# A conformer/short-conv block on eight cores: twenty token tiles transposed by DMA instead of TensorE, a gate computed one stage later, bias adds split in two

## What is computed

```
shift1, scale1, gate1, shift2, scale2, gate2 = split(silu(c) @ w_ada + b_ada)
h  = LN(x) * (1 + scale1) + shift1
a_val, a_gate, b_gb, b_gc, b_x, g_a, g_b = split(h @ w_in + b_in)        # 7 x 1024 columns
u  = silu(LN(conv31(a_val * sigmoid(a_gate))));   y_a = u @ w_a_out + b_a_out
v  = b_gb * conv3(b_gc * b_x);                    y_b = v @ w_b_out
x1 = LN(alpha * x + (1 + gate1) * ((sigmoid(g_a) * y_a + sigmoid(g_b) * y_b) @ w_o + b_o))
h2 = LN(x1) * (1 + scale2) + shift2
y  = LN(alpha * x1 + (1 + gate2) * (relu(h2 @ w_up + b_up)^2 @ w_down + b_down))
```

## Time and profile before

| | |
|---|---|
| median of 3 runs | 1168.89 us (1168.38 to 1169.64) |
| the profiled execution's own time | 1170.01 us |
| its span (core 4, the slowest) | 1169.0 us |
| spans of the eight cores | 1155.9 to 1169.0 us |
| PE, DVE, ACT, POOL busy | 94%, 58%, 37%, 15% of the span |

### The profile page before, as it was taken

The page is one execution under the profiler, slowest core; times in us unless marked ns, Lnnn a source line. Parts: engine busy times, 40 slices in busy tenths (PEclk is TensorE's granted clock), DMA queues, the critical chain, the costliest instruction groups (busy, mean ns, idle before and its releaser), DMA issues.

```text
span 1169.0 us, 19292 instructions; the slowest of 8 cores (1155.9 to 1169.0 us)
## 1 busy us (share of the span) xinstructions
PE 1102.7 (94%) x6607; PEld 577.5 (49%) x6676; DVE 677.8 (58%) x1159; ACT 437.2 (37%) x773; POOL 175.1 (15%) x159
## 2 busy tenths in 40 slices
PE   1699999979999999999999999999999999999896
PEld 1366776434445677644444444444444444444343
DVE  4548766827653267588877767877032782210566
ACT  2344436824442234584466644456000043320000
POOL 4004011002100000111321021210060000003300
PEclk9999999989999999999999999999999999999898
DMA  9999998998555652498763685636944399654412
GB/s 189 179 138 127 136 158 116 207 188 162 74 73 93 110 90 34 60 182 160 127 127 85 132 148 117 130 75 139 223 72 72 72 187 239 106 81 74 73 56 89
DMA packets 150335, 143.14 MB, mean 122 GB/s; under 512 B 33840, under 2 KB 138688, under 8 KB 149984
## 3 DMA queue, kind: packets, MB, share of 16 engines
q0 software_dynamic: 106736, 87.73, 53.9%
q1 hardware_dynamic: 43504, 54.18, 16.7%
HBM read 203.22 MB, written 16.79 MB: 188 GB/s over the span
## 4 chain that ended last, share of the span: by engine, by line
PE 80%; DMA 6%; DVE 5%; issue 3%; ACT 3%; SPq 2%; POOL 2%; DVEq 0%; ACTq 0%; POOLq 0%
PE bank L161 79%; DMA wb<-w_in 4%; SPq L138 2%; ACT nb L1063 2%; DMA wb<-w_down 1%; POOL x1r L1286 1%; PE bank L531 1%; DVE cbuf L1055 1%; DMA u<-nb 1%; DVE slot L500 1%; DVE fT L1236 0%; ACT sg L1135 0%; DVE x L664 0%; DVE sg L1138 0%; POOL wb L138 0%
## 5 line engine op out<-in xcount | busy, mean ns | idle before, releaser
L161 PE MATMUL bank<-hT,wb 128*128 128x512 bf16 (+4 forms) x2112 | 387.9, 337 | 1.9 <-ACT sg L1135 1.3
L161 PEld LDWEIGHTS bank<-hT,wb 128*128 128x128 bf16 x2112 | 202.2, 98 | 156.8 <-issue 13.9
L161 PE MATMUL bank<-h2T,wb 128*128 128x512 bf16 x1002 | 222.8, 379 | 3.1 <-DVE x L664 1.9
L161 PE MATMUL bank<-wb,fT 128*128 128x512 bf16 x941 | 209.2, 381 | 5.4 <-DMA wb<-w_down 4.4
L161 PEld LDWEIGHTS bank<-h2T,wb 128*128 128x128 bf16 x1024 | 99.5, 98 | 121.5 <-issue 2.9
L161 PEld LDWEIGHTS bank<-wb,fT 128*128 128x128 bf16 x960 | 94.0, 98 | 118.7 <-issue 6.2
L1234 ACT ACTIVATE rr<-bank,pvec 128x512 bf16<-128x512 f32 x128 | 85.1, 683 | 111.1 <-PE bank L161 108.9
L1236 DVE TENSOR_TENSOR fT<-rr 128x512 bf16<-128x512 bf16 x128 | 63.4, 513 | 91.0 <-ACT rr L1234 91.0
L505 ACT ACTIVATE slot<-slot,eps 128x1 f32<-128x1 f32 (+1 forms) x65 | 17.6, 290 | 253.9 <-DVE slot L502 240.2
L1254 DVE TENSOR_TENSOR gt<-bank,g2b 128x512 f32<-128x512 f32 x32 | 21.9, 683 | 123.1 <-PE bank L161 123.1
L138 POOL DMA_DIRECT2D wb<-w_in x40 | 36.0, 925 | 326.3 <-PE bank L161 305.5
(11 more groups left out here) (116 smaller groups left out, 1180.8 us busy)
## 6 DMA issues: line engine op xcount, KB each, us to landing
wb<-w_in POOLq DMA_DIRECT2D x16, 1024.0 KB, 13.3
wb<-w_up POOLq DMA_DIRECT2D x16, 1024.0 KB, 13.2
wb<-w_down POOLq DMA_DIRECT2D x15, 1024.0 KB, 9.9
wada<-w_ada POOLq DMA_DIRECT2D x12, 1024.0 KB, 18.8
wb<-w_in POOLq DMA_DIRECT2D x24, 512.0 KB, 19.6
xt<-xs SPq DMA_DIRECT2D x16, 512.0 KB, 9.7
x<-xs SPq DMA_DIRECT2D x16, 512.0 KB, 5.0
x1d<-x SPq DMA_DIRECT2D x16, 512.0 KB, 3.2
```

The costliest lines, as they stand in the source:

```text
L161: inst = pe.h.matmul(out, lhsT, rhs, start=self.first, stop=last)
```

## The change

1. The 8 tiles of block 1's `hT` and tiles 0 to 5 of each block's `h2T` (20 of the 24) are transposed by one DMA each, issued on SP with `transpose=True`, from the normalised tile in SBUF straight to its place. Scale and shift are applied later, in place, by `modulate_tiles`: 5 DVE and 3 ACT instructions over a group of 3 tiles (`hT`) or 2 tiles (`h2T`). Tiles 6 and 7 of each `h2T` stay as they were. Block 1's `hT` loses its gaps, so its columns are read as one run.
2. The first weight tile of each `up` runs over tokens 0 to 511 for its four column groups and then over tokens 512 to 1023.
3. Gate 2 moves: its two `w_ada` loads to step 0 of block 1's GLU, `ada_gate` to step 14, `ada_rows` to step 16, `ada_spread` and the scaling of `b_down` to step 20.
4. In both `down`, tiles 4 to 7 get their bias at `gq == 1` and tiles 0 to 3 at `gq == 2`.

```diff
     def ada_rows(i_):
+        off = (OFF_BC, OFF_TMP + 15872)[i_]
+        grow, r_grow = sb(off, [8, 128], F32, "grow"), newres("grow%d" % i_, off, 512)
...
+    def modulate_tiles(hT, r_hT, t0, t1, sc, sh, rm):
+        for kc in range(KC):
+            view = hT[:, kc, t0 * 128:t1 * 128]
+            x_ = 0 if kc < 5 else 1
+            rw = [r_hT[t][x_] for t in range(t0, t1)]
+            if kc < 5:
+                dve.op(lambda e: e.tensor_scalar(view, view, modT[:, sc + kc:sc + kc + 1], modT[:, sh + kc:sh + kc + 1], ALU.mult, ALU.add),
+                       reads=rw + [rm], writes=rw)
+            else:
+                act.op(lambda e: e.activation(view, view, AF.Identity, bias=modT[:, sh + kc:sh + kc + 1], scale=modT[:, sc + kc:sc + kc + 1]),
+                       reads=rw + [rm], writes=rw)
...
+    def dma_transpose(dst, src, owner, reads, writes):
+        sp.deps(reads, writes)
+        if owner.dsem is None:
+            fw.nsem += 1
+            owner.dsem = nc.alloc_semaphore("d%d_%s" % (fw.nsem, owner.name))
+        owner.dcnt += 16
+        sp.h.dma_start(out=dst, in_=src, transpose=True).then_inc(owner.dsem, 16)
...
         def trans(i):
             npart, ri, dv = tiles[i]
+            if not raw:
+                dma_transpose(hT[:, :, i * 128:(i + 1) * 128], xn[i % nxn], own("tr%d" % (i % nxn)), [r_xn[i % nxn]], r_hT[ri])
+                return
...
+        def mod(g):
+            modulate_tiles(hT, r_hT[1:], 3 * g, min(3 * g + 3, NT), SC1, SH1, r_mod1)
...
         def trans(t):
-            transpose_evac(h2n[t % 2], 128, r_h2n[t % 2], h2T, r_h2T[t], lambda dst, kc: dst[:, kc, t * 128:(t + 1) * 128],
-                           (SC2, SH2, r_mod2), n_dve)
...
+            if t >= 6:
+                transpose_evac(h2n[t % 2], 128, r_h2n[t % 2], h2T, r_h2T[t], lambda dst, kc: dst[:, kc, t * 128:(t + 1) * 128],
+                               (SC2, SH2, r_mod2), n_dve)
+                return
+            dma_transpose(h2T[:, :, t * 128:(t + 1) * 128], h2n[t % 2], own("tr2_%d" % (t % 2)), [r_h2n[t % 2]], r_h2T[t])
+
+        def mod(i):
+            modulate_tiles(h2T, r_h2T, 2 * i, 2 * i + 2, SC2, SH2, r_mod2)
...
         def hcols(kc, s):
+            if b > 0:
+                return hT[:, kc, s * 512:(s + 1) * 512]
             return hT[:, kc, :].rearrange("p (r n) -> p r n", n=PW)[:, 4 * s:4 * s + 4, PW - NPH:PW]
+
+        def hbank(ap):
+            return ap if b > 0 else grp4(ap)
...
+            def hin(kc):
+                return cols(hT, kc) if b == 0 else hT[:, kc, r0_ * 128:r1_ * 128]
...
-                grp.mm(view(bank_ap[bi]), wa[:, kc, jj * 128:(jj + 1) * 128], cols(hT, kc), [ra[jj // 2]] + rd, last=(kc == KC - 1))
+                grp.mm(bank_ap[bi][:, 0:n], wa[:, kc, jj * 128:(jj + 1) * 128], hin(kc), [ra[jj // 2]] + rd, last=(kc == KC - 1))
...
         n_ = 0
         for g in range(8):
             wu, ru, iu = ws_get()
-            for jj in range(4):
+            for jj, s in ([(jj, s) for s in range(NS) for jj in range(4)] if g == 0 else [(jj, s) for jj in range(4) for s in range(NS)]):
                 fc = 4 * g + jj
-                for s in range(NS):
+                if True:
...
         for gq in range(4):
             wd, rd, idn = ws_get()
-            if gq == 2:
-                for t in range(NT):
-                    x1_bias(t)
-                if last:
+            if gq in (1, 2):
+                for t in range(4):
+                    x1_bias(t if gq == 2 else t + 4)
+                if last and gq == 2:
                     wl, rl = sb(OFF_H[1], [128, 8, 512], BF16, "wl"), newres("wl", OFF_H[1], 8192)
                     dma_group(pool, [(wl, wsrc(w_down, 3 * 1024, 512))], own("wl"), writes=[rl])
...
+        if n in (7, 14):
+            n0 = {7: 6, 14: 8}[n]
             for nt in (n0, n0 + 1):
                 ada_load(nt, OFF_H[1] + (nt % 2) * 8192, "h%d" % (nt % 2))
...
-        if n == 11:
+    plan = Plan()
+
+    def scaled_bias(c_, dst, gb_, rg_, off):
+        bst, r_bst = sb(off, [128, D], F32, "bstage"), newres("bst", off, 4096)
+        sp.dma(bst, bc_d[:, c_:c_ + 1024], own("bst"), writes=[r_bst])
+        pool.op(lambda e: e.tensor_tensor(dst, bst, gb_, ALU.mult), reads=[r_bst, rg_], writes=[r_bias])
+
+    def glu1_side(n):
+        if n == 0:
+            for nt in (10, 11):
+                ada_load(nt, OFF_CB + (nt % 2) * 8192, "h%d" % (nt % 2))
+        elif n == 14:
             ada_gate(1)
-        if n == 12:
+        elif n == 16:
             ada_rows(1)
-        if n == 15:
+        elif n == 20:
             ada_spread(1)
-
-    plan = Plan()
+            scaled_bias(5120, bdb, g2b, r_g2, OFF_TMP + 6144)
...
         r_bc2 = newres("bc", OFF_BC, 8192)
         sp.dma(bc, bc_d[:, 0:2048], own("bc"), writes=[r_bc2, r_bc])
-        bst = sb(OFF_TMP + 12288, [128, D], F32, "bstage")
-        r_bst = newres("bst", OFF_TMP + 12288, 4096)
-        for c_, dst, gb_, rg_ in ((4096, bob, g1b, r_g1), (5120, bdb, g2b, r_g2)):
-            sp.dma(bst, bc_d[:, c_:c_ + 1024], own("bst"), writes=[r_bst])
-            pool.op(lambda e: e.tensor_tensor(dst, bst, gb_, ALU.mult), reads=[r_bst, rg_], writes=[r_bias])
+        scaled_bias(4096, bob, g1b, r_g1, OFF_TMP + 12288)
...
@@ -1397,9 +1449,10 @@
                     plan.add(9 * g + 2 * i, pp["stats"], t)
                     plan.add(9 * g + 5, pp["root"], t)
                     plan.add(9 * g + 6 + 2 * i, pp["norm"], t)
-                    plan.add(9 * g + 8 + 2 * i, pp["trans"], t)
+                    plan.add(9 * g + 7 + 2 * i, pp["trans"], t)
                 if t + 6 < NT:
                     plan.add(9 * g + 7 + 2 * i, pp["load"], t + 6)
+            plan.add(min(9 * g + 14, 30), pp["mod"], g)
...
         plan.add(0, scale_wo, 15)
-        p3_plan(pp, 2, 3, (1, 2, 4, 5, 7))
-
-    def p3_plan(pp, first, step, lags):
+        p3_plan(pp, 2, 3, (1, 2, 4, 5, 7), 4)
...
             for lag, key in zip(lags, ("root1", "ln1", "root2", "ln0", "trans")):
                 plan.add(n + lag, pp[key], t)
+            if t % 2 == 1 and t < 6:
+                plan.add(n + lags[4] + mlag, pp["mod"], t // 2)
             if t + nx < NT:
                 plan.add(n + lags[3], pp["load"], t + nx)
...
-    mg1, r_mg1 = token_mix(1, side["P1"], OFF_H[0], OFF_CB + 16384, no_side, no_side, gb1_side, plan.run, after_gb1)
+    mg1, r_mg1 = token_mix(1, side["P1"], OFF_H[0], OFF_CB + 16384, glu1_side, no_side, gb1_side, plan.run, after_gb1)
     plan.done()
...
-    p3_plan(H2[1], 4, 6, (2, 4, 7, 9, 13))
+    p3_plan(H2[1], 4, 6, (2, 4, 7, 9, 13), 9)
     fT, r_fT = up(0, H2[0]["h2T"], H2[0]["r_h2T"], plan.run)
...
```

More of the change, by code:

```diff
@@ L595, in x_ring @@
         return slot, load
+    def modulate_tiles(hT, r_hT, t0, t1, sc, sh, rm):
[16 more added lines that the diff above has]
+        sp.h.dma_start(out=dst, in_=src, transpose=True).then_inc(owner.dsem, 16)
+        ev = (owner.dsem, owner.dcnt, "dma_" + owner.name)
+        for r in reads:
+            r.r["dma_%s_%d" % (owner.name, owner.dcnt)] = ev
+        for w in writes:
+            w.w = ev
+            w.r = {}
     def p1_setup(b, ring, xn_offs, raw, n_dve):
-        hT = sb(OFF_H[b], [128, KC, TW], BF16, "hT")
+        hT = sb(OFF_H[b], [128, KC, TW if raw else TB], BF16, "hT")
         _g = new_group(fw, ["hT%d_%d%s" % (b, t, ab) for t in range(NT + 1) for ab in "ab"], OFF_H[b], OFF_H[b] + HSZ)
@@ L631, in trans @@
             npart, ri, dv = tiles[i]
+            if not raw:
+                dma_transpose(hT[:, :, i * 128:(i + 1) * 128], xn[i % nxn], own("tr%d" % (i % nxn)), [r_xn[i % nxn]], r_hT[ri])
+                return
             transpose_evac(xn[i % nxn], npart, r_xn[i % nxn], hT, r_hT[ri], dv, None if raw else (SC1, SH1, r_mod1), n_dve)
-        return dict(hT=hT, r_hT=r_hT, load=load, stats=stats, root=root, norm=norm, trans=trans, n=len(tiles))
+        def mod(g):
+            modulate_tiles(hT, r_hT[1:], 3 * g, min(3 * g + 3, NT), SC1, SH1, r_mod1)
+        return dict(hT=hT, r_hT=r_hT, load=load, stats=stats, root=root, norm=norm, trans=trans, mod=mod, n=len(tiles))
     def p3_setup(b, mg, r_mg, wo, x1_offs, h2n_offs, n_dve):
@@ L688, in trans @@
         def trans(t):
-            transpose_evac(h2n[t % 2], 128, r_h2n[t % 2], h2T, r_h2T[t], lambda dst, kc: dst[:, kc, t * 128:(t + 1) * 128],
-                           (SC2, SH2, r_mod2), n_dve)
-        return dict(h2T=h2T, r_h2T=r_h2T, load=load, bias=bias, proj=proj, root1=root1, ln1=ln1, root2=root2, ln0=ln0, trans=trans, nx1=nx1)
+            if t >= 6:
[5 more added lines that the diff above has]
+            modulate_tiles(h2T, r_h2T, 2 * i, 2 * i + 2, SC2, SH2, r_mod2)
+        return dict(h2T=h2T, r_h2T=r_h2T, load=load, bias=bias, proj=proj, root1=root1, ln1=ln1, root2=root2, ln0=ln0, trans=trans, mod=mod, nx1=nx1)
     class Plan:
@@ L908, in pair @@
             for kc in range(KC):
```

(7 more changed lines are left out.)

11 lines of the change are left out of this document (3 added, 8 removed).

## The result

The changed kernel takes **1153.01 us** (median of 4 runs, 1152.17 to 1153.36) against 1169.27 of the kernel before (4 runs, 1168.38 to 1170.01). The ratio is 0.986, with a 95% interval of 0.9843 to 0.9877: faster, by 16.3 us. The forecast was 1145 and a gain of 23.6. The time lies inside the range of 1139 to 1163, but 2 us above the likeliest case (1139 to 1151), in the band that the prediction gave to rival (a), that the holes close only in part. Only fast runs are compared, those in which neither die fell to a lower clock than the other; one run of the kernel before at 1189.37 us still counts as fast and lowers the ratios of one chip, that of the repeat and the three kernels after it, by some 0.2%.

A forecast was written before the change was run, and what follows sets the result against it. TensorE, busy 94% of the span, was taken as the bound. Transposes 9.0, gate 7.7, bias adds 6.9, `up` 1.0, less 1.0 for XC, gave 23.6: 1170.0 to 1146.4, median 1145 us; range 1139 to 1163.

The forecast's parts named there:

- rival (a): The holes at the first `u` group and last `down` close only in part: about 15 us gained, 1154; chance 0.2.
- the stall for `u` and what follows: Block 0's first `u` group: 6.0 us hole plus 1.9 of slow clock go, less 1.5 for late pieces.
- row matmuls and gate: TensorE's wait ahead of the row matmuls before block 0's merge goes with gate 2's move: 1.3 us.
- wait in XC: Start of block 1's XC: ACT may wait for staging bytes shared with `cbf`; cost 1.0 us, bounds 0 and 4.
- bias adds: Last `down`: last weights load 4.6 us sooner, closing a 4.44 us hole and its 2.5 us after-effect; 6.9 us.
- The gate's step: Taking gate 2's 2.1 MB from ahead of the `u<-nb` pieces shortens the queue by 12 us, against a 6.04 us hole.
- Rival (b): Slow DMA transposes stall TensorE, from 10.4 us a tile in block 0's merge, 13.8 beside `w_o`; 1216 at 16; chance 0.12.
- 20 tiles x 0.45 = 9.0 us: Both merges and `up(0)`: each tile not transposed on TensorE saves 0.45 us of path, 9.0 us in all.
- The first goes with DVE's evictions: `up(0)`: TensorE's 1.9 us wait for `x` goes, its 0.8 us wait for `h2n` stays; 1.0 us booked.
- The check on core 5: Core 5's 1160.6 us less 9.0, 1.3 and some 5 for its smaller holes gives 1145, agreeing with the forecast.
- rival (c): New waits of many kinds eat the gains up to nothing, within 0.2%; chance 0.03.

The follow-up runs named there:

- the repeat: The changed kernel run again, unaltered, on the chip of the next three kernels: ratio 0.9838, median 1156.81 us.
- the three kernels after it: The changed kernel with gate 2's staging load, row and multiplication earlier (1155.67 us), with `h2T` scaling later (1152.83), and with the two together (1151.39).
- the doubled run: The changed kernel with every transposing DMA issued twice, SP waiting for the first: 1168.99 us, ratio 0.9957.
- both edits: The changed kernel with gate 2's staging load, row and multiplication earlier and `h2T` scaling later in merge 1 and `up(0)`: 1151.39 us, ratio 0.9791.
- The last run: Against the kernel with both edits, seven instead of three of a tile pair's eight scale-and-shift instructions on ScalarE in `up(0)`: 1148.54 us, ratio 0.979.

## Why the prediction was nearly right, and where it failed

The table sets the terms against core 4, the core for which they were worked out.

| term | booked | measured on core 4 |
|---|---|---|
| transposes, 8 tiles in block 0's merge | 3.6 | 3.6 |
| transposes, 6 tiles in merge 1 | 2.7 | 0.5 |
| transposes and `x` waits, `up(0)` | 3.7 | 1.5 |
| the stall for `u` and what follows | 6.4 | 8.1 |
| row matmuls and gate (GB of block 0, GLU of block 1) | 1.3 | 0.6 |
| wait in XC | -1.0 | -0.4 |
| bias adds | 6.9 | 7.1 |
| sum | 23.6 | 21.0 |

- **The gate's step was right.** The stall is gone on every core of the changed kernel, and the groups behind it keep 1.73 us. The two terms of block 0's merge add to the 11.7 us of the stage table and are split by the run with the gate alone (8.1) and the two runs with and without `hT` (3.6). The 1.5 us kept back for late pieces weren't needed.
- **The bias adds were right**: 60.43 us up to `wl` is 280 matmuls at 0.216, without a hole. The margin of the last load was booked as 0.65 us, with 16 us to land; it landed in 12.8 on core 7, 3.9 us ahead of its use.
- **A DMA transpose** takes 5.0 to 5.1 us by the medians of core 7 (3.8 to 5.6 over the cores), against 6 taken from the pace of the `u<-nb` pieces; the ends of 1.6 and 39 us were far off. No engine waits for one. By the 1309 ns for one 128x128 block of the Trainium skill, "VectorE: DVE Perf Modes", section "The three transpose paths", a tile of eight would take 10.5 us, an estimate. By the 261 GB/s of the Trainium skill, "DMA: Bandwidth & Descriptors", section "Latency and other measured facts", it would take about 1 us, also an estimate. Both miss the median; 10.6 and 11.2 us were seen in the crowd, 3.0 at the least.
- **Rival (b)'s threshold** left something out. Behind the place of the scaling it gave TensorE three steps of free banks, 10.4 us. Measured are 4.9: the 28.3 us that TensorE bears less the 23.4 at which the scaling stands. The rows of the doubled run fit with that: when the scaling is late, ScalarE has 2.30 us of it, two table loads and the square roots to do, 5.6 us from 306.10 to 311.67, before it reads the next bank, and three steps of 3.45 us less 5.6 leave 4.8. The 10.4 us a tile "without end" was a pace over many groups; no run measured that.
- **The step that failed:** "20 tiles x 0.45 = 9.0 us, and this is path, since TensorE has no slack there". The price of 0.45 is exact, and eight tiles gave it in full. For twelve it went again into new holes, because the scaling that comes back in was costed at nothing ("covered by those engines' spare time"). On core 4, merge 1 won 2.7 us and lost 2.1 to a hole that it did not have; `up(0)` won 2.7, but where three holes of 2.7 us in all had been, one of 2.3 us now stands, and the clock of 0.72 behind it costs some 1.7 more (16 matmuls from 754.74 to 759.88 us take 5.1 instead of 3.45). The spare time is an average over stages. In merge 1 the cover was there but the place wrong: 2.3 us of VectorE ahead of the chain that tile 7 needs; moved two steps, the whole 2.7 us came (130.39). In `up(0)` the cover isn't there. VectorE is busy 103.1 of 142 us there even with both edits, in one chain with ScalarE and the banks, and the DMA took only 0.9 us of work from it (24 evictions, 8.2 us before; 5.2 us of scaling and 2.1 of evictions after). It is GpSimd's additions that make VectorE the bound, as the run without them shows: 139.03 us and no hole. The last run agrees: 12 scalings less on VectorE shorten the stage by 3.35 us.
- **"The first goes with DVE's evictions"** failed with it: the waits on `x` grew from 1.9 to 5.1 us.
- **The check on core 5** (1160.6 less 15.3) failed for the same reason. Core 5 got 8.6 us in block 0's merge in all, 2.1 in the last `down` and 0.5 in merge 1, and lost 1.0 in `up(0)`, 0.7 in XC and 0.5 at the start: 9.0, so that it ended at 1151.6.
- **Not booked at all:** a stage that was equal on all cores and becomes uneven costs the slowest core more than the mean. XC (up to +2.3), `up(0)` (2.5 between cores) and the start (2.8 us later on core 7 than in the execution before, by nothing that the change touched) came together on core 7. The clock behind the new holes belongs here too: it fell on some cores, for 1.7 us each time. Between the 1146.4 forecast for the profiled execution and its own time of 1153.36 lie 7.0 us: 2.6 are core 4's missing terms, 4.3 its distance to core 7 (1152.3 - 1148.0).
- **Luck:** the range was wide enough because rival (a) was in it, and (a) is not what happened. The time came into its band by the twelve tiles and the uneven stages, neither of which was among the rivals with a price of its own; rival (c), new waits, was priced only as eating the whole gain, at 0.03.

The share of each part: gate 0.67%, bias adds 0.52%, `hT` by DMA some 0.4% (0.9886 to 0.9845; by the stage lengths 3.6 us, 0.3%), `h2T` by DMA nothing as placed, and 2.7 us in merge 1 once the scaling stands elsewhere. The other token order in the first weight tile of `up` shows nothing: with it (all transposes on TensorE) and without it (the gate alone) `up(0)` takes 144.60 and `up(1)` 110.5.
